# Moving one of four one-hot rows per gate group from VectorE to GpSimd

## The reference

```
def block(ub):                                   # a block of 128 tokens
    q = (ub @ P['peer_wq']).reshape(t, 8, 2, 128)
    s = einsum('thpd,pkd->thpk', q, P['peer_subkeys'])
    sv, si = lax.top_k(s, 16)
    cand = (sv[:, :, 0, :, None] + sv[:, :, 1, None, :]).reshape(t, 8, 256)
    top, ci = lax.top_k(cand, 16)
    e = take(si[:, :, 0], ci // 16) * 128 + take(si[:, :, 1], ci % 16)
    gate = softmax(top)                          # 8 x 16 = 128 picks per token
    act = gelu(einsum('tkd,td->tk', P['peer_u'][e], ub))
    return einsum('tk,tkd->td', gate * act, P['peer_v'][e])
```

## Time and profile before

| what | value |
|---|---|
| median of three runs | 6208.47 us (6203.03 to 6233.56) |
| the profiled execution, its own time | 6228.09 us |
| span of that execution | 6226.5 us |
| busy, of the span | PE 85%, DVE 60%, ACT 24%, POOL 24% |
| opening's groups, layer 0 | 1689 to 2088 us, 96 groups |
| opening's groups, layer 1 | 5014 to 5229 us, 64 groups |
| row on DVE (L1587) | x480, median 341 ns |
| row on POOL (L1339) | x160, median 823 ns |

### The profile page before, as it was taken

The page is one execution under the profiler, slowest core; times in us unless marked ns, Lnnn a source line. Parts: engine busy times, 40 slices in busy tenths (PEclk is TensorE's granted clock), DMA queues, the critical chain, the costliest instruction groups (busy, mean ns, idle before and its releaser), DMA issues.

```text
span 6226.5 us, 64675 instructions
## 1 busy us (share of the span) xinstructions
PE 5310.1 (85%) x22991; PEld 3572.5 (57%) x22991; DVE 3707.7 (60%) x8308; ACT 1464.0 (24%) x3638; POOL 1473.6 (24%) x1540
## 2 busy tenths in 40 slices
PE   8899888786787799999999589987796846999997
PEld 3699644554663455555555379944473745666664
DVE  1545252744886688887665465416373697775665
ACT  1100021312276412112111210003221165111111
POOL 0000000000024555445553000000000036434552
PEclk9899989678897799999999789998757956999998
DMA  6000000001357899999997100010001438999996
GB/s 219 21 1 1 24 17 27 8 20 62 119 197 274 346 418 414 401 405 404 399 413 299 49 4 1 1 37 7 31 1 42 141 123 328 415 418 412 417 417 272
DMA packets 292960, 1184.08 MB, mean 190 GB/s; under 512 B 24736, under 2 KB 106912, under 8 KB 207392
## 3 DMA queue, kind: packets, MB, share of 16 engines
q0 software_dynamic: 92160, 671.13, 26.4%
q1 hardware_dynamic: 194864, 455.59, 20.0%
q10 hardware_dynamic: 5616, 53.23, 2.1%
HBM read 1130.57 MB, written 49.28 MB: 189 GB/s over the span
## 4 chain that ended last, share of the span: by engine, by line
PE 65%; DVE 18%; DMA 10%; ACT 3%; issue 2%; POOL 2%; ACTq 0%; SPq 0%; DVEq 0%; POOLq 0%
PE psum L510 64%; DMA arena<-in_ut 6%; DVE arena L1376 3%; DMA arena<-gate_blocks 2%; DMA x_tokens<-in_uv,arena 1%; DVE arena L1706 1%; DVE arena L1515 1%; DVE arena L1781 1%; DVE arena L1385 1%; DMA arena<-in_uv,arena 1%; DVE arena L1513 1%; ACT arena L1001 1%; DVE arena L1379 1%; DVE arena L1587 1%; ACT y_features L1077 1%
## 5 line engine op out<-in xcount | busy, mean ns | idle before, releaser
L510 PE MATMUL psum<-arena 128*128 128x64 f32 (+7 forms) x8416 | 1550.1, 361 | 46.0 <-DVE arena L1706 23.9
L510 PE MATMUL psum<-u_features,weight_ring 128*128 128x256 f32 (+2 forms) x4672 | 1319.7, 439 | 36.7 <-ACT arena L1106 18.3
L510 PEld LDWEIGHTS psum<-arena 128*128 128x128 f32 (+2 forms) x8416 | 1082.8, 213 | 397.3 <-issue 279.5
L510 PEld LDWEIGHTS psum<-u_features,weight_ring 128*128 128x128 f32 x4672 | 896.7, 194 | 454.4 <-issue 240.0
L1354 POOL TENSOR_TENSOR arena<-consts 128x1 f32<-128x1 f32 x640 | 334.9, 523 | 1264.4 <-DVE y_features L1610 1092.3
L510 PE MATMUL psum<-u_features,arena 128*128 128x384 f32 (+1 forms) x2048 | 588.1, 442 | 39.3 <-DMA arena<-in_ut 35.6
L1001 ACT ACTIVATE arena<-psum 128x512 f32<-128x512 f32 (+5 forms) x404 | 250.6, 620 | 1543.1 <-PE psum L510 1313.2
L510 PE MATMUL psum<-weight_ring,consts 128*128 128x512 f32 x1280 | 570.3, 592 | 0.0
L510 PEld LDWEIGHTS psum<-u_features,arena 128*128 128x128 f32 x2048 | 396.7, 195 | 253.9 <-issue 56.5
L1355 POOL DMA_INDIRECT arena<-in_uv,arena x350 | 485.3, 1387 | 99.3 <-POOL arena L1354 93.5
L1112 ACT ACTIVATE arena<-arena 128x1 f32<-128x1 f32 x640 | 129.8, 203 | 1485.4 <-DVE arena L1602 1482.3
(11 more groups left out here) (201 smaller groups left out, 5437.2 us busy)
## 6 DMA issues: line engine op xcount, KB each, us to landing
weight_ring<-in_ws SPq DMA_DIRECT2D x250, 512.0 KB, 3.6
weight_ring<-in_ut SPq DMA_DIRECT2D x128, 512.0 KB
weight_ring<-in_uv SPq DMA_DIRECT2D x128, 512.0 KB
arena<-in_ut SPq DMA_DIRECT2D x128, 512.0 KB
arena<-in_uv SPq DMA_DIRECT2D x128, 512.0 KB
gate_blocks<-arena ACTq DMA_DIRECT2D x20, 2048.0 KB, 7.8
arena<-gate_blocks SPq DMA_DIRECT2D x32, 768.0 KB, 18.9
arena<-gate_blocks SPq DMA_DIRECT2D x32, 512.0 KB, 27.2
```

What stands on the lines that cost most here:

```text
L510: return pe.matmul(o, w, x, start=first, stop=last, skip_group_check=True)
```

## The change

Of the four side rows of every group, DVE makes the rows 0 and 1 (before: 0, 1 and 2), and POOL makes 2 and 3 (before: 3). The operation, its operands and the semaphores stay; the mark that PE waits for stands on the last row of each engine. No other instruction changes, and the planner's list of events is the same.

```
-                    i = QUAD * q + 3
-                    done.free(pool.tensor_scalar(SIDE[k % 4][:, 3 * P:4 * P], cf(K_IOTA), TURN[d % 2][:, P + i:P + i + 1],
-                                                 TURN[d % 2][:, i:i + 1], ALU.is_equal, ALU.mult), "last sides", l, k)
+                    for j in range(2, QUAD):
+                        i = QUAD * q + j
+                        done.free(pool.tensor_scalar(SIDE[k % 4][:, j * P:(j + 1) * P], cf(K_IOTA), TURN[d % 2][:, P + i:P + i + 1],
+                                                     TURN[d % 2][:, i:i + 1], ALU.is_equal, ALU.mult), "last sides", l, k)
...
-                for j in range(3):
+                for j in range(2):
                     i = QUAD * q + j
                     done.free(dve.tensor_scalar(SIDE[k % 4][:, j * P:(j + 1) * P], cf(K_IOTA), TURN[d % 2][:, P + i:P + i + 1],
                                                 TURN[d % 2][:, i:i + 1], ALU.is_equal, ALU.mult), "sides", l, k)
```

## The result

The changed kernel took 6252.75 us, the median of 20 runs (6231.32 to 6280.35). The kernel before, run beside it 20 times, took 6217.38 us. The ratio is 1.0057, with a 95% interval of 1.0040 to 1.0075: 0.57% or about 35 us slower, between 25 and 47. The forecast was +19 us and 6228 us, with a range of 6202 to 6262 us for the time.

What follows compares the result with a forecast made beforehand. VectorE was taken to bound the early parts, TensorE layer 0's middle, GpSimd's queue and DRAM waits layer 1's late part. Terms -2 + 0 - 4 + 17 + 8 = +19 us gave about 6228 us; own range 6216 to 6240, 8-in-10 range 6202 to 6262.

Steps and rivals of the forecast that it cites:

- Layer 1, early: Layer 1's early part: ScalarE's waiting limits what VectorE's 9.4 us can give; -4 us, ends -9 and 0.
- the prediction's sign: Layer 1's early part in the changed profile: shorter by some 4 us, ScalarE at about 95%, VectorE below it.
- Layer 0, first tile: Layer 0's early part, to 1733 us: 4.0 us off VectorE, limited by ScalarE's idle time; -2 us, ends -4 and 0.
- Layer 1, late: Layer 1's late part: 32 more GpSimd rows, partly absorbed by 14.8 us of slot waits; +17 us, ends +10 and +33.
- Layer 0, late: Layer 0's late part: 35 more GpSimd rows, 41.4 us, against 33.4 us of slot waits; +8 us.
- all filled up: Layer 0's late part: added rows use all 33.4 us of GpSimd's waits for slots, leaving +8 us.
- Two terms at nothing: Layer 0, 1733 to 1925 us, where GpSimd's waits cover 39 us of rows, and the block loops: each priced at 0.
- the loop starts as much later as the opening ends, and its work is the same: Loop over the blocks behind the opening: it only shifts with the opening's end, adding nothing of its own.
- rival B: Late parts: nothing absorbed, each fetch later by a full row; up to +68 us, about +50 with free tails; chance 0.22.
- Within 0.5%: Whole kernel: the change stays within the 31 us that a measurement can't tell from no change; chance 0.67.
- A: Late parts: GpSimd has room, idle time takes the rows, early gain is left; -13 to +5 us; chance 0.17.
- C: Late parts: GpSimd's rows hold up VectorE's long instructions; up to +35 us with the forecast, 6243 us; chance 0.08.

## Why the prediction was right, and where it fell short

**The mechanism** was the one forecast, stage by stage: GpSimd's queue gets longer, and in the late parts what waits for it has no slack. One row added on GpSimd alone gives the late tiles to 0.5 us (the kernel with two rows in the last tiles alone was 3.8 and 2.4 us below), and VectorE's relief alone is worth nothing in layer 1's. The prediction followed the cost through the late fetch only; after the change TensorE's groups wait for GpSimd too, and with them ScalarE's weights.

**Layer 1, early**: -4 forecast, -4.2 measured, -4.7 by relief alone. The bound taken was not VectorE's 9.4 us but ScalarE's waits, and that agrees: ScalarE is busy for 86.8 us of the tile before and 86.5 us after, 95% of it, as the prediction's sign had it, with VectorE at 85.6 us. **Layer 0, first tile**: -2 forecast, -1.3 and, in the kernel without late rows, 0.

**Layer 1, late**: +17 forecast, +19.4 measured. That it came so near is in part luck, since two errors nearly cancel. The rows cost 47.2 us more (33.15 to 80.38), not 33.2: a row became 1.26 us, not 1.04. But the prediction held everything else in GpSimd's queue fixed, and the rest, mostly the issues, became 17.7 us shorter, of which the two issues fewer in the window are about 3. GpSimd's busy time grew by 29.5 us (96.59 to 126.08) and its idle time fell by 9.5, from 25.4 of 122 us to 15.9 of 142. The waits for slots, less the first, went from 14.8 us to 7.1 (16.0 less 8.9), and not to nothing. GpSimd was to be busy for over 90% and was for 89%.

**Layer 0, late**: +8 forecast, +13.2 measured. This is the term that was mis-sized, and the step that failed is "all filled up": it was worked out as if all 33.4 us of GpSimd's waits could take rows. The tile before and after, columns as in the earlier trace rows:

```profile
1948.70:2089.00 140.30, 93.09 (x360) 58.26 (x360) 92.43 (x177) 98.24 (x256) 91.63 (x86) 0.70 0.89 343
1961.50:2115.00 153.50, 94.11 (x360) 58.91 (x360) 85.68 (x145) 98.61 (x256) 126.26 (x118) 0.68 0.79 302
```

GpSimd is busy for 34.6 us more (its rows 39.7 us, the rest 5.1 less), and its idle time fell from 48.7 to 27.2 us, by 21.5 and not by 33.4. A likely reason, which no run tried alone, is that TensorE's modulation pieces let four groups and four slots come at once: within such a bunch GpSimd is full, and the idle time between the bunches comes too late for them.

**Two terms at nothing were not nothing.** Layer 0's second tile cost 2.6 us, and 1.2 us in the kernel without late rows, though 85.2 us of waits stood against 39 us of work; at 1.2 us that is within the spread of an untouched tile. And the step "the loop starts as much later as the opening ends, and its work is the same" failed: layer 0's loop grew by 6.2 us. Layer 1's 2.1 us are hardly more than the 1.6 us that a kernel with no more late work showed there. VectorE's first wait in the loops, in the kernel before, layer 0 and then layer 1:

```profile
DVE consts L1597 <- DMA arena<-gate_blocks: 20.0, 1, 20.0
...
DVE consts L1597 <- DMA arena<-gate_blocks: 15.3, 1, 15.3
```

In the changed kernel:

```profile
DVE consts L1598 <- DMA arena<-gate_blocks: 26.0, 1, 26.0
...
DVE consts L1598 <- DMA arena<-gate_blocks: 24.5, 1, 24.5
```

GpSimd ends the opening with the rows of the last six groups in one block, and three fetches stand behind it:

```profile
2096.24 12.65 POOL L1340 TENSOR_SCALAR arena<-consts 128x128 f32<-128x128 f32 x12
2108.86 0.18 POOL L1355 TENSOR_TENSOR arena<-consts 128x1 f32<-128x1 f32 x1
2109.32 1.04 POOL L1356 DMA_INDIRECT x_tokens<-in_uv,arena  x1 [0.28 <-POOL arena L1355]
```

They are issued from 2109 to 2113 us, right ahead of the last 2 MB store at 2114.99. Before, they went out from 2078 to 2083 us, with the store at 2088.97. Three megabytes of rows now move beside the store. The chain of waits shows which transfer became longer; the last store of layer 0 and the first load of its gates, before and then after (start, length):

```profile
2088.97 8.14 DMA gate_blocks<-arena
2097.20 4.90 DMA arena<-gate_blocks
2114.99 12.92 DMA gate_blocks<-arena
2128.00 4.73 DMA arena<-gate_blocks
```

The store takes 4.8 us more and the load no more. In the four kernels with a longer GpSimd queue in the last tiles the last store of a layer takes 12.1 to 14.2 us and VectorE's wait is 23 to 26 us in both layers. In the others the store takes 6.2 to 8.4 us where the chain names it, but for layer 0 of the kernel with VectorE's relief alone: there it takes 11.2 us, and that loop is 3.0 us longer. So in layer 0 the longer loops are those with the longer store. That the three fetches are what lengthens it was not tried by itself.

**The sum** was +19 where the stages show +38: +7.6 in the two late tiles, +8.3 in the loops, +2.6 in the second tile, and 0.5 in the first tiles. As a difference, +35 us by runs, the result lies about halfway between the forecast and rival B, whose +50 us, with nothing absorbed, was too much. The time lies within the range given, 6202 to 6262 us, but outside the forecast's own, 6216 to 6240. Of the 25 us between 6228 and 6252.75, 9 are not the change's: the kernel before had a median of 6217.38 us in 20 runs, where the forecast started from 6208.47 in three. "Within 0.5%" had 0.67, and 0.57% came out (0.40 to 0.75). Of the rivals, A is refuted by every kernel with late rows; its price was also added up wrongly, as -9 - 4 and 0 to +10 give -13 to -3 and not to +5. C is refuted by VectorE's medians, 1225 and 1282 ns against 1218 and 1279. The mean side row in the late parts was to be near 1.1 us and was 1.26 and, in layer 0, 78.49 / 64 = 1.23.

The half of the rule in the Trainium skill's page "SBUF — State Buffer", section "Who interferes with whom", by which a GpSimd instruction that reads SBUF is held up by VectorE's two-input instructions while one that only writes is not, agrees with the rows: reading rows reach 2862 ns from 780, the memset 322 from 195. Of the other half, that VectorE is held up in turn, the rows show little: beside twice the side rows the dot product has a median of 1225 ns and a maximum of 1572, the weighted sum 1282 and 1385.

## What to carry to other kernels

Where an engine's queue holds both small compute and the issue of transfers that others wait for, the compute is priced at the transfer: count the time from issue to issue, not the engine's busy share over the whole span. Don't hold the issues' own length fixed either: it was 1.79 us in the median before and 1.04 after. A split of work between two engines can be right in one stage and wrong in the next; here 2:2, 3:1 and 4:0 by stage beat both fixed splits that were measured, 3:1 and 2:2; 4:0 throughout was not. Idle time covers an addition only if it stands ahead of the same deadline: of 33.4 us of waits in layer 0's third tile 21.5 us were used.

## What the runs showed of the hardware

The issue of an indirect DMA held GpSimd for anything from 1.03 to 2.24 us in layer 1's late part before the change, median 1.79, and for 1.04 us in the median after it. In the kernel with no row on GpSimd there, the same issue took this (ns min/median/max):

```profile
L1359 POOL DMA_INDIRECT x_tokens<-in_uv,arena x20: 1023/1028/1031, 5115.5 to 5212.9; - x20
```

There each issue starts 0.5 us behind the end of GpSimd's wait for VectorE's sum, and so at the same phase of VectorE's work. That the phase is what shortens it is inferred from the two timelines, and was not tried alone.

The stretch between the layers, which no edit touches, differed by up to 33 us between the ten profiles (1572.3 to 1605.8 us), as much as the change itself, and TensorE's busy time accounts for it within 1.3 us, longer at a lower granted clock. The clock goes with the time of whole executions too: runs of the kernel before at a mean granted clock of 0.879 to 0.881 took 6230 to 6245 us, and those at 0.887 and 0.888 took 6196 to 6207. Tiles that an edit doesn't touch repeated to half a microsecond in most profiles, at the worst to 1.5.
